# Five accumulator banks instead of four in the stages of Block 3

## The reference, cut to what matters

```python
def layer_norm(x, g, b):
    xf = x.astype(jnp.float32)
    mu = xf.mean(-1, keepdims=True)
    var = jnp.square(xf - mu).mean(-1, keepdims=True)
    return ((xf - mu) * lax.rsqrt(var + LN_EPS) * g + b).astype(x.dtype)

def swiglu(x, w_in, w_out):
    gate, up = jnp.split(x @ w_in, 2, axis=-1)
    return (jax.nn.silu(gate) * up) @ w_out

for i in range(2):
    x = layer_norm(ALPHA * x + 0.5 * swiglu(x, *ffn1), *ln1)
    mix = chunked_gmlp(x, *mixer) if i == 0 else nsa(x, *mixer)
    x = layer_norm(ALPHA * x + mix, *ln2)
    x = layer_norm(ALPHA * x + 0.5 * swiglu(x, *ffn2), *ln3)
```

## Time and profile before

| what | value |
|---|---|
| median of 3 runs | 2637.76 us (2636.64 to 2644.43) |
| span of the profiled execution, first to last instruction | 2643.0 us |
| DVE busy, ACT busy | 50%, 35% of the span |
| mean granted PE clock | 0.979 of full |
| Block 3's first-unit matmuls | from about 1497 us |

### The profile page before, as it was taken

The page is one execution under the profiler, slowest core; times in us unless marked ns, Lnnn a source line. Parts: engine busy times, 40 slices in busy tenths (PEclk is TensorE's granted clock), DMA queues, the critical chain, the costliest instruction groups (busy, mean ns, idle before and its releaser), DMA issues.

```text
span 2643.0 us, 39144 instructions
## 1 busy us (share of the span) xinstructions
PE 2496.3 (94%) x16618; PEld 1762.0 (67%) x16618; DVE 1329.3 (50%) x1846; ACT 913.3 (35%) x1243; POOL 261.3 (10%) x181
## 2 busy tenths in 40 slices
PE   7988999999989999879999999999999999999998
PEld 5652323333323333278899899998899999887997
DVE  4451222212223222188777755756665765785755
ACT  4441111111111111056555544553444444435443
POOL 3000000000000000021000101262011201202200
PEclk9999999999999999989999999999999999999999
DMA  9689999999999999953455566555466466451562
GB/s 335 212 311 425 427 428 406 427 428 427 428 423 414 427 428 428 427 182 132 152 199 192 183 207 208 178 172 191 163 223 208 159 208 207 136 171 38 177 210 103
DMA packets 248986, 713.68 MB, mean 270 GB/s; under 512 B 12563, under 2 KB 186345, under 8 KB 223910
## 3 DMA queue, kind: packets, MB, share of 16 engines
q1 hardware_dynamic: 237424, 690.26, 68.8%
q10 hardware_dynamic: 9446, 15.97, 1.8%
q0 software_dynamic: 1936, 4.87, 0.6%
HBM read 710.01 MB, written 1.05 MB: 269 GB/s over the span
## 4 chain that ended last, share of the span: by engine, by line
PE 51%; DVE 3%; ACT 2%; issue 1%; POOL 0%; DVEq 0%; ACTq 0%; POOLq 0%
PE bank L429 19%; PE bank L671 13%; PE bank L434 10%; PE bank L623 4%; PE bank L703 2%; ACT ap L3945 1%; PE bank L899 1%; PE bank L2680 1%; PE bank L3456 0%; PE bank L467 0%; DVE stats L3219 0%; DVE xa L3217 0%; PE bank L4025 0%; ACT hi L362 0%; PE bank L3759 0%
## 5 line engine op out<-in xcount | busy, mean ns | idle before, releaser
L371 DVE TENSOR_TENSOR lo<-ring,hi 128x2048 fp32r<-128x2048 f32 x251 | 601.8, 2403 | 249.1 <-ACT hi L362 248.8
L362 ACT ACTIVATE hi<-ring 128x2048 fp32r<-128x2048 f32 x251 | 476.0, 1900 | 136.3 <-PE bank L671 106.8
L2130 PE MATMUL bank<-expert,xg 128*64 128x512 f32 x1664 | 387.6, 604 | 29.0 <-DMA expert<-in_w_mlp 28.1
L429 PE MATMUL bank<-x_hi,hi 128*128 128x256 f32 (+1 forms) x1576 | 369.1, 279 | 0.0
L429 PE MATMUL bank<-x_lo,hi 128*128 128x256 f32 (+1 forms) x1576 | 366.7, 278 | 0.0
L429 PEld LDWEIGHTS bank<-x_hi,hi 128*128 128x128 f32 (+1 forms) x1576 | 296.1, 188 | 3.3 <-issue 1.8
L429 PEld LDWEIGHTS bank<-x_lo,hi 128*128 128x128 f32 (+1 forms) x1576 | 296.0, 188 | 2.2 <-issue 0.7
L2130 PEld LDWEIGHTS bank<-expert,xg 128*64 128x64 f32 x1664 | 114.0, 137 | 241.7 <-issue 208.0
L2260 DVE TENSOR_TENSOR acc<-bank,acc 128x512 f32<-128x512 f32 x100 | 62.1, 683 | 332.7 <-PE bank L2238 332.6
L434 PE MATMUL bank<-x_hi,lo 128*128 128x256 f32 (+1 forms) x1576 | 197.0, 278 | 0.9 <-DVE lo L371 0.9
L2213 PE MATMUL bank<-expert,aT 128*64 128x512 f32 x832 | 185.7, 596 | 5.5 <-DMA expert<-in_w_mlp 5.5
(11 more groups left out here) (697 smaller groups left out, 3908.5 us busy)
## 6 DMA issues: line engine op xcount, KB each, us to landing
expert<-in_w_mlp SPq DMA_DIRECT2D x192, 2048.0 KB, 18.9
ring<-in_l_ffn_w_in SPq DMA_DIRECT2D x88, 1024.0 KB, 5.1
ring<-in_l_ffn_w_out SPq DMA_DIRECT2D x44, 1024.0 KB, 4.9
ring<-in_w_ada SPq DMA_DIRECT2D x24, 1024.0 KB, 7.0
ring<-in_l_gm_w_in SPq DMA_DIRECT2D x24, 1024.0 KB, 5.2
ring<-in_ffn_w_up SPq DMA_DIRECT2D x22, 1024.0 KB, 5.1
ring<-in_w_in SPq DMA_DIRECT2D x21, 1024.0 KB, 7.4
ring<-in_l_gm_w_out SPq DMA_DIRECT2D x12, 1024.0 KB, 4.9
```

Source lines behind the costliest of these rows:

```text
L362: e.activation(k.half("hi", u), k.slot(j), ACT.Copy).then_inc(*k.up("hi_done"))
L371: e.tensor_tensor(k.half("lo", u), k.slot(k.units[u][0]), k.half("hi", u).bitcast(F32), SUB).then_inc(*k.up("lo_done"))
L429: e.matmul(o, l, r, start=fresh, stop=False, skip_group_check=True)
L2130: i = e.matmul(banks[n][j][h * CAP:(h + 1) * CAP, :], x, W[:, (2 * h + j) * 512:(2 * h + j + 1) * 512], start=c == 0, stop=False, skip_gro ...
```

## The change

The held sums get five banks: (0,0) and (0,1) of 512 columns for token half 0, (1,0) of 512, (1,1) and (1,2) of 256 columns for token half 1. `rows_pe` becomes `fifths_pe` and `last_rows_pe` becomes `last_fifths_pe` in the stages of Block 3. In the last two units the part (1,0) now goes before the second-last unit's products for the last half. DVE sums (1,0) before it finishes half 0's moments, takes half 1's statistics in four pieces of 256 columns, and sums (1,1) and (1,2) apart. `norm_act` no longer calls `split_act`. The tile `stats` grows from 24 to 36 floats and the filler `edge` shrinks by 16. The mixers `gm` and `nsa` get the same replacements as `ffn3_pe`; they are left out below.

```diff
@@ -693,15 +693,45 @@
             m.then_inc(*(k.USED() if b + h == 2 else k.MM(nm, "acc", b, h)))
 
 
-def last_rows_pe(k, e, nm, acc, us, xs, ready):
+FIFTHS = ((0, 0, 0, 512), (0, 1, 512, 512), (1, 0, 0, 512), (1, 1, 512, 256), (1, 2, 768, 256))
+
+
+def fifth_banks(k, e, nm):
+    return {(b, h): k.bank(e, nm, "acc", b, h, hold=True) for b, h, _, _ in FIFTHS}
+
+
+def fifths_free(k, nm):
+    for b, h, _, _ in FIFTHS:
+        k.release(nm, "acc", b, h)
+
+
+def fifths_pe(k, e, acc, u, xhi, xlo, first):
+
+    hi, lo = k.half("hi", u), k.half("lo", u)
+    fresh = {q: first for q in acc}
+    e.wait_ge(*k.hi_at(u))
+    for w, xs in ((hi, (xhi, xlo)), (lo, (xhi,))):
+        if w is lo:
+            e.wait_ge(*k.lo_at(u))
+        for c in range(2):
+            for side in range(2):
+                for x in xs:
+                    for b, h, a, n in FIFTHS:
+                        if b == side:
+                            m = e.matmul(acc[b, h][:, 0:n], x[:, c, b * 128:(b + 1) * 128], w[:, c, a:a + n], start=fresh[b, h], stop=False, skip_group_check=True)
+                            fresh[b, h] = False
+    m.then_inc(*k.USED())
+
+
+def last_fifths_pe(k, e, nm, acc, us, xs, ready):
 
     def part(i, b, h):
         hi, lo = k.half("hi", us[i]), k.half("lo", us[i])
         xhi, xlo = xs[i]
+        a, n = [(a, n) for d, g, a, n in FIFTHS if (d, g) == (b, h)][0]
         for c in range(2):
             for w, x in ((hi, xhi), (hi, xlo), (lo, xhi)):
-                m = e.matmul(acc[b, h][:, :], x[:, c, b * 128:(b + 1) * 128], w[:, c, h * 512:(h + 1) * 512],
-                             start=False, stop=False, skip_group_check=True)
+                m = e.matmul(acc[b, h][:, 0:n], x[:, c, b * 128:(b + 1) * 128], w[:, c, a:a + n], start=False, stop=False, skip_group_check=True)
         return m
 
     def come(i):
@@ -713,11 +743,12 @@
     for b, h in ((0, 0), (0, 1), (1, 0)):
         part(0, b, h)
     come(1)
-    for h in range(2):
-        part(1, 0, h).then_inc(*k.MM(nm, "acc", 0, h))
-    part(0, 1, 1).then_inc(*k.USED())
-    part(1, 1, 0).then_inc(*k.MM(nm, "acc", 1, 0))
-    part(1, 1, 1).then_inc(*k.USED())
+    for b, h in ((0, 0), (0, 1), (1, 0)):
+        part(1, b, h).then_inc(*k.MM(nm, "acc", b, h))
+    part(0, 1, 1)
+    part(0, 1, 2).then_inc(*k.USED())
+    part(1, 1, 1).then_inc(*k.MM(nm, "acc", 1, 1))
+    part(1, 1, 2).then_inc(*k.USED())
 
 
 def heads_pe(k, e, nm, sqs, lhs):
@@ -3204,25 +3235,29 @@
     for h in range(2):
         cols = slice(h * 512, (h + 1) * 512)
         e.activation(t["unit"][:, 0, cols], t["xa"][:, 0, cols], ACT.Identity, bias=mv[:, 0, 2:3], scale=mv[:, 0, 1:2]).then_inc(*k.ACT(nm, "unit", 0, h))
-    split_act(k, e, u + 3)
     std(1)
     upper_act(k, e, nm, gain, bias, t["x_hi"])
 
 
 def sums_dve(k, e, nm, u, scale, b, h):
 
-    t, cols = k.t, slice(h * 512, (h + 1) * 512)
-    xa = t["xa"][:, b, cols]
-    e.wait_ge(*(k.used(u) if b + h == 2 else k.mm(nm, "acc", b, h)))
-    e.scalar_tensor_tensor(xa, k.got(nm, "acc", b, h)[:, :], scale, xa, MUL, ADD).then_inc(*k.DVE(frees=(nm, "acc", b, h)))
-    e.wait_ge(*k.dve())
-    e.bn_stats(t["stats"][:, b, h, :], xa).then_inc(*k.DVE())
+    t = k.t
+    a, n = [(a, n) for d, g, a, n in FIFTHS if (d, g) == (b, h)][0]
+    xa = t["xa"][:, b, a:a + n]
+    e.wait_ge(*(k.used(u) if h == 2 else k.mm(nm, "acc", b, h)))
+    e.scalar_tensor_tensor(xa, k.got(nm, "acc", b, h)[:, 0:n], scale, xa, MUL, ADD).then_inc(*k.DVE(frees=(nm, "acc", b, h)))
+    e.wait_ge(*k.dve())
+    if b:
+        for j in range(n // 256):
+            e.bn_stats(t["stats"][:, 2 + a // 256 + j, :], xa[:, j * 256:(j + 1) * 256]).then_inc(*k.DVE())
+    else:
+        e.bn_stats(t["stats"][:, h, :], xa).then_inc(*k.DVE())
 
 
 def mean_dve(k, e, nm, b):
     t, mv = k.t, k.t["moments"]
     e.wait_ge(*k.dve())
-    e.bn_aggr(mv[:, b, 0:2], t["stats"][:, b, :, :].rearrange("p a b -> p (a b)")).then_inc(*k.DVE(nm, "var", b))
+    e.bn_aggr(mv[:, b, 0:2], flat(t["stats"][:, 2:6, :] if b else t["stats"][:, 0:2, :])).then_inc(*k.DVE(nm, "var", b))
 
 
 def rstd_dve(k, e, nm, b):
@@ -3244,10 +3279,11 @@
     sums_dve(k, e, nm, u, scale, 0, 0)
     sums_dve(k, e, nm, u, scale, 0, 1)
     mean_dve(k, e, nm, 0)
+    sums_dve(k, e, nm, u, scale, 1, 0)
     rstd_dve(k, e, nm, 0)
     shift_dve(k, e, nm, 0)
-    sums_dve(k, e, nm, u, scale, 1, 0)
     sums_dve(k, e, nm, u, scale, 1, 1)
+    sums_dve(k, e, nm, u, scale, 1, 2)
     mean_dve(k, e, nm, 1)
     rstd_dve(k, e, nm, 1)
     e.wait_ge(*k.dve())
@@ -3350,14 +3387,14 @@
             for half in range(2):
                 unit_mm(k, e, k.bank(e, nm, i, half), ups[i][half], t["x_hi"], t["x_lo"])
         if i == 1:
-            acc = acc_banks(k, e, nm)
+            acc = fifth_banks(k, e, nm)
         if 0 < i < NFF - 1:
             s = (i - 1) % 2
             e.wait_ge(*k.dve((nm, i - 1), "lo", 0))
-            rows_pe(k, e, nm, acc, downs[i - 1], t[f"act_hi{s}"], t[f"act_lo{s}"], i == 1, False)
-    last_rows_pe(k, e, nm, acc, downs[-2:], [(t[f"act_hi{i % 2}"], t[f"act_lo{i % 2}"]) for i in (NFF - 2, NFF - 1)],
+            fifths_pe(k, e, acc, downs[i - 1], t[f"act_hi{s}"], t[f"act_lo{s}"], i == 1)
+    last_fifths_pe(k, e, nm, acc, downs[-2:], [(t[f"act_hi{i % 2}"], t[f"act_lo{i % 2}"]) for i in (NFF - 2, NFF - 1)],
                  [((nm, i), "lo", 0) for i in (NFF - 2, NFF - 1)])
-    acc_free(k, nm)
+    fifths_free(k, nm)
 
 
 def ffn3_act(k, e, nm, ln):
...
@@ -4119,8 +4156,8 @@
 
 def lay_block3(k, ctx):
     A = k.A
-    k.sb("rows", [128, 2, DM], F32, ctx), k.sb("stats", [128, 2, 2, 6], F32, ctx)
-    k.sb("edge", [128, 88], F32, ctx)
+    k.sb("rows", [128, 2, DM], F32, ctx), k.sb("stats", [128, 6, 6], F32, ctx)
+    k.sb("edge", [128, 72], F32, ctx)
     for i in range(2):
         k.sb(f"act_hi{i}", [128, 2, 256], F32R, ctx), k.sb(f"act_lo{i}", [128, 2, 256], F32R, ctx)
     for i in range(2):
```

More of the change, by code:

```diff
@@ L3460, in gmlp_pe @@
         project(i)
-    acc = acc_banks(k, e, "gm")
+    acc = fifth_banks(k, e, "gm")
     for i in range(12):
@@ L3468, in gmlp_pe @@
             e.wait_ge(*k.dve(("gm", i - 1), "lo", 0))
-            rows_pe(k, e, "gm", acc, k.gm_out[i - 1], t[f"act_hi{s}"], t[f"act_lo{s}"], i == 1, False)
-    last_rows_pe(k, e, "gm", acc, k.gm_out[10:], [(t[f"act_hi{i % 2}"], t[f"act_lo{i % 2}"]) for i in (10, 11)],
+            fifths_pe(k, e, acc, k.gm_out[i - 1], t[f"act_hi{s}"], t[f"act_lo{s}"], i == 1)
+    last_fifths_pe(k, e, "gm", acc, k.gm_out[10:], [(t[f"act_hi{i % 2}"], t[f"act_lo{i % 2}"]) for i in (10, 11)],
                  [(("gm", i), "lo", 0) for i in (10, 11)])
-    acc_free(k, "gm")
+    fifths_free(k, "gm")
     meet(k, e, PE_, "gm")
@@ L4058, in nsa_pe @@
             job_values_pe(k, e, x - 3)
-    acc = acc_banks(k, e, "nsa")
+    acc = fifth_banks(k, e, "nsa")
     for i in range(2):
         e.wait_ge(*k.dve("no_parts", "lo", i))
-        rows_pe(k, e, "nsa", acc, k.first["nsa_out"] + i, pair(k.t["x_hi"], i), pair(k.t["x_lo"], i), i == 0, False)
-    last_rows_pe(k, e, "nsa", acc, [k.first["nsa_out"] + i for i in (2, 3)], [(pair(k.t["x_hi"], i), pair(k.t["x_lo"], i)) for i in (2, 3)],
+        fifths_pe(k, e, acc, k.first["nsa_out"] + i, pair(k.t["x_hi"], i), pair(k.t["x_lo"], i), i == 0)
+    last_fifths_pe(k, e, "nsa", acc, [k.first["nsa_out"] + i for i in (2, 3)], [(pair(k.t["x_hi"], i), pair(k.t["x_lo"], i)) for i in (2, 3)],
                  [("no_parts", "lo", i) for i in (2, 3)])
-    acc_free(k, "nsa")
+    fifths_free(k, "nsa")
     meet(k, e, PE_, "nsa")
```

## The result

The changed kernel takes **2685.47 us** (median of 4 runs, 2682.69 to 2686.76) against 2637.36 (4 runs, 2636.64 to 2644.43) for the kernel before: ratio 1.0181, 95% interval 1.0166 to 1.0196, 48 us slower. The forecast was 2667 with a range of 2654 to 2682: the direction was right, the size was not, and the measured time lies above the range.

The account below looks back on a forecast made before the run. It took the matmul engine, busy 94% of the span, as the bound. Terms 21.3 + 0.4 - 0.7 + 8.5 - 5.2 = +24.3 on the 2643.0 span, or +29.5 on the 2637.76 median without the -5.2, gave 2667 us, range 2654 to 2682.

Parts of the forecast that it names:

- Part 1, the moved split: At Block 3's five seams PE waits for the next stage's second weight unit, now split behind all x_hi: +21.3 us.
- 2096.68: At the 2088 seam, the predicted start in us of the first-unit matmuls behind the moved split; 2091.99 before.
- Part 5, the dips: At each of five seams PE's clock drops to 1.2 GHz for 3.4 us, losing 1.7 us: +8.5 us in all.
- Part 2, the sums: DVE's sums and statistics at a seam: half 1's aggregate comes 0.30 us earlier, with 0.20 taken at 1901.
- Part 3, the last norm: At the last norm, already bound by DVE, splitting the sums and one extra statistics add 0.4 us.
- Parts 4 and 5, the pace: Matmuls in Block 3: 360 pairs of 256 columns give -0.7 us, short pace in more FFN stages gives -5.2 us.
- the pace argued in part 5: FFN stages behind a dip run at the short pace, so each 256-column pair costs -1.9 ns, not +6.0.
- all seams dip: If all five seams dip, the stage from 2088 gains 4.2 us and units after 1678 and 2449 gain 1.0: -5.2.
- The tie between dip and pace: At five seams of the trace, two with a dip are followed by the short pace, three without by the long.
- the long pace everywhere: Rival: the mixed 512 and 256 pattern sets the long pace in three or four FFN stages, about 2684 us; chance 0.08.
- The Trainium skill's price of a split: For the 360 pairs in down units, one more fixed 2.5 ns per split, an estimated +0.9 us.

Follow-up runs that it names:

- e11: Changed kernel with token half 1's matmuls ordered 256, 512, 256 columns and first_units_pe called with ahead=False; 2638.3 us, ratio 1.0003 to the kernel before.
- e2_split_only: Kernel before with only the split_act call taken out of norm_act; 2664.0 us, ratio 1.0095.
- e14_four_between: Kernel before, four banks, token half 1's products as 256, 512, 256 columns in all but each stage's last two down units; iterations 16.45 us, no total time given.
- e4_mix_only: Kernel before, four banks, (1,1) product made as two 256-column matmuls in all but the last two down units of Block 3; 2657.7 us, ratio 1.0060.
- e8: Kernel before with (1,1) products as two 256-column matmuls in each FFN stage's first down unit alone; iterations about 16.87, 16.50, then 16.40 us, no total time given.
- e3: Changed kernel with split_act back in norm_act and token half 1's two 256-column matmuls before its 512-column one; 2660.3 us.
- e9: Changed kernel with split_act back in norm_act and token half 1's matmuls ordered 256, 512, 256 columns; 2644.4 us, ratio 1.0025 to the kernel before.
- e5: Changed kernel with split_act back in norm_act and each down unit's 512-column matmuls first, its twelve 256-column ones last; 2653.3 us, ratio 1.0052 to the kernel before.
- e12: Kernel before, four banks, with the split left out of norm_act and first_units_pe called with ahead=False; ratio 1.0018.
- e13: Kernel before, four banks, token half 1's products as 256, 512, 256 columns in the first down unit of each Block 3 stage alone; 2639.5 us, ratio 0.9991.

## Why the prediction was wrong

**Part 1, the moved split: right.** The wait stands at each of the five seams, before L623, 5.2 us and 6.4 at the one with the loads. The step "2096.68" had the matmuls start 4.69 us later than 2091.99; from the last sums matmul the first L623 is 9.03 us off instead of 4.44, 4.59 later. Forecast with the dips 21.3 + 8.5 = 29.8 us over five seams, measured 30.9.

**Part 5, the dips: right in kind, a little too small.** At the 2088 seam the 96 matmuls take 13.00 us in the chain where the long pace without a dip gives 11.47 (3 x 3.77 + 0.16), so 1.5 us there; 1.7 was forecast. By the windows the clock was at the lower level twice as long as the 3.4 taken, some 6.8 us ((0.29 + 0.50 + 0.06) x 4 / 0.5), but half of that passed while PE waited. That seam has the smallest part behind the wait. Over the five seams 21.6 us of matmuls lay at the lower level, which at half rate costs 10.8 us, where 8.5 was forecast. The Trainium skill (TensorE: Matmul & The Clock Gate, HAM oscillation) has gaps between bursts of matmuls bring the clock down, and the trace agrees: 0.71 in the window from 2112, in which PE did 0.10 us of work in 4, and 0.50 in the next.

**Part 2, the sums: right.** The rows gave 0.42 and 0.43 for the 256-column sum and statistics, as taken. From half 0's aggregate to half 1's it is 3.77 us (2105.79 to 2109.56) where it was 4.11 (2085.32 to 2089.43): 0.34 earlier for a forecast of 0.30, and 0.06 of it goes to the longer aggregate (0.27 for 0.21). Where nothing else stands in the way a seam gains 0.4 us (e11).

**Part 3, the last norm: nearly right.** From half 0's aggregate (2631.95, now 2672.72) to half 1's (2637.39, now 2678.42) it is 5.44 and 5.70 us, 0.3 longer; I had +0.4.

**Parts 4 and 5, the pace: wrong, and this is the step that failed.** The text took -0.7 us for the 360 pairs, "for the pace argued in part 5", and -5.2 us because "all seams dip". Measured is +13.2 us over the iterations. (Taken from the median, where the forecast left the -5.2 out, +29.5 was forecast and +48.1 measured.) Between the two profiles +24.3 was forecast and +41.1 measured, 16.8 apart. This term alone is 13.2 + 5.9 = 19.1 apart and the seams 1.1; against them stand 3.5 us for the rest (-3.1 for +0.4). Two things went wrong in it. The tie between dip and pace was read from five seams, two against three, and e2_split_only shows a dip with the long pace behind it. And a pair was priced by its own length, while most of its cost lies in the up units behind it. Of the 0.48 us that an iteration is longer (16.40 to 16.88), 0.40 lies in its 96 up matmuls, which have not changed at all and go at 0.1178 instead of 0.1134; the down unit itself takes 5.57 for 5.49, some 13 ns for each of its six pairs, where -1.9 or +6.0 was taken. The rival "the long pace everywhere", at 2684, described what happened; I had given it 0.08. It should have had more, because the kernel before had the long pace in one of four stages without any mix, so the pace was known not to be safe. The range ended two microseconds below that rival's figure, and the measured time lies 3.5 us above the range.

**The Trainium skill's price of a split** (TensorE: Matmul & The Clock Gate, Back-to-back issue gap: an estimated +0.9 us by its fixed part per matmul) misses it as well: e14_four_between, with the same count of narrow matmuls, adds 0.05 us per iteration, e4_mix_only 0.48, and nothing in a sum per instruction tells these apart.

## What to carry to other kernels

Before an operation is moved behind a group, look who waits for its counter at the head of the next stage: the wait for the second weight unit stood right above the loop that it held up, and 1.9 us of work moved by 7 us cost 25 (e2_split_only). Price a change of matmul shape by the stream that follows it, not by the matmuls that are changed: try the orders of the same matmuls, and read start-to-start times of the untouched ones. And a tie seen in five places of one trace is a guess: where a term hangs on it, the range must hold both signs.

## What the runs showed of the hardware

A stream of equal matmuls, here 128x256 in the rounded float32 format, each with its own weight load, goes at one of two start-to-start times with the clock at full: 0.1134 or 0.1178 us, 4% apart. Either can last through units and whole stages, and the long one can also end after one plain unit (e8). It is set by what went before, and reproducibly so where widths are mixed. Of the groups of three behind one stationary operand, 512, 256, 256 and 256, 256, 512 lead to the long pace (e4, e3), 256, 512, 256 to the short one with four banks and with five (e14, e9), and twelve narrow ones at a unit's end flip it at every unit (e5). Wide ones alone hold either (16.40 and 16.82 in the kernel before). Part of the spread of the kernel before from run to run may come from this: the profiles with its down units unchanged have the long pace in `l1_ffn1` (before, e12) or in `l1_ffn2` (e2). Another part may be the dips: with four banks and the split in place, two to four of the five seams have one (two before and in e13, three in e14, four in e4 and e8). Neither was shown run by run. What in PE holds the state is open. In the trace of the kernel before, the records of the up units come in the same order at either pace and differ in this: from the start of a weight load to the start of its matmul it is 110 ns for nearly all at the short pace and 114 to 116 at the long, and at the long pace a quarter of the weight loads takes 192 ns, which none does at the short, where they take 187 or 188. From the start of a matmul to the next weight load it is 2 to 5 ns at either.
